# The gate of eight tokens a step moves from VectorE's one-hot columns into GpSimd's one-hot rows

## What is computed

```python
top_s, pos = lax.top_k(cand, PEER_TOPK)
eidx = jnp.take_along_axis(cidx, pos, axis=-1)          # i1 * 128 + i2
gate = jax.nn.softmax(top_s, axis=-1).astype(x.dtype)
...
hidden = jax.nn.gelu(jnp.einsum('td,thkd->thk', xb, u_tab[eb]))
return jnp.einsum('thk,thkd->td', gb * hidden, v_tab[eb])
```

## Time and profile before

| | |
|---|---|
| median of 3 runs | 3813.95 us (3813.29 to 3815.09) |
| the profiled execution | 3812.06 us |
| its span, first to last instruction | 3810.1 us |
| TensorE busy | 3728.1 us |
| VectorE busy | 2730.8 us |
| ScalarE busy | 1487.8 us |
| GpSimd busy | 1284.5 us |
| granted TensorE clock, mean | 0.996 |
| spreading stage, layer 1 | 953.0 to some 1097 us |
| spreading stage, layer 2 | 2846.2 to some 2991 us |

### The profile page before, as it was taken

How to read it: one execution, slowest core, us unless ns; L and a number is a source line. 1 busy time by engine, 2 the same in 40 slices (tenths; PEclk the granted TensorE clock), 3 DMA queues, 4 the chain that set the end, 5 groups by cost and what they waited for, 6 DMA issues and landing times. The chain is left out here.

```text
span 3810.1 us, 53339 instructions
## 1 busy us (share of the span) xinstructions
PE 3728.1 (98%) x19506; PEld 3310.0 (87%) x19506; DVE 2730.8 (72%) x5347; ACT 1487.8 (39%) x2154; POOL 1284.5 (34%) x1040
## 2 busy tenths in 40 slices
PE   8999999999999999999999999999999999999998
PEld 7878888999999999988878788889999899999887
DVE  3257635499989888878642566355999888888887
ACT  2244522244763333333322445223447533333332
POOL 1000000265856555544000000002658556555440
PEclk9999999999999999999999999999999999999999
DMA  4212423254689999999732225233537899999995
GB/s 148 101 56 75 161 91 138 108 184 157 216 287 382 358 355 348 344 346 354 257 133 94 65 68 171 78 139 112 206 142 229 302 378 357 358 350 344 342 357 208
DMA packets 321524, 847.59 MB, mean 222 GB/s; under 512 B 21056, under 2 KB 119360, under 8 KB 296256
## 3 DMA queue, kind: packets, MB, share of 16 engines
q1 hardware_dynamic: 247616, 576.84, 42.9%
q0 software_dynamic: 73728, 268.47, 18.8%
HBM read 755.58 MB, written 89.65 MB: 222 GB/s over the span
## 5 line engine op out<-in xcount | busy, mean ns | idle before, releaser
L93 PE MATMUL bank<-xT_low,u_high 128*128 128x384 f32 (+1 forms) x2144 | 728.9, 340 | 11.5 <-ACT hid L1897 7.3
L95 PE MATMUL bank<-xT_high,u_low 128*128 128x384 f32 (+1 forms) x2144 | 723.4, 337 | 0.0
L94 PE MATMUL bank<-xT_high,u_high 128*128 128x384 f32 (+1 forms) x2144 | 723.1, 337 | 0.0
L93 PE MATMUL bank<-v_low,w_high 128*128 128x512 f32 x1536 | 597.7, 389 | 0.9 <-DVE v_low L1998 0.9
L95 PE MATMUL bank<-v_high,w_low 128*128 128x512 f32 x1536 | 598.2, 389 | 0.0
L94 PE MATMUL bank<-v_high,w_high 128*128 128x512 f32 x1536 | 598.1, 389 | 0.0
L1189 POOL TENSOR_TENSOR u_low<-merged,u_high 128x1024 fp32r<-128x1024 f32 x96 | 243.1, 2546 | 1043.8 <-ACT u_high L1184 1043.6
L1257 POOL DMA_INDIRECT far_rows<-peer_v_dram,far_index x256 | 389.3, 1521 | 415.3 <-DVE x_far L1281 369.5
L1257 POOL DMA_INDIRECT far_rows<-peer_u_rows_dram,far_index x256 | 374.8, 1464 | 312.6 <-DVE far_dots L1263 259.7
L1998 DVE TENSOR_TENSOR v_low<-v_raw,v_high 128x1024 fp32r<-128x1024 f32 x256 | 301.8, 1221 | 207.4 <-ACT v_high L1909 207.3
L1909 ACT ACTIVATE v_high<-v_raw 128x1024 fp32r<-128x1024 f32 x256 | 257.3, 1052 | 472.2 <-PE bank L95 467.2
(11 more groups left out here) (445 smaller groups left out, 6811.3 us busy)
## 6 DMA issues: line engine op xcount, KB each, us to landing
merged<-peer_u_dram SPq DMA_DIRECT2D x128, 1024.0 KB, 7.7
v_raw<-peer_v_dram SPq DMA_DIRECT2D x128, 1024.0 KB, 9.4
gates_scratch<-stage SPq DMA_DIRECT2D x24, 2048.0 KB, 8.3
G<-gates_scratch SPq DMA_DIRECT2D x64, 768.0 KB
hidden_scratch<-ahead_hid SPq DMA_DIRECT2D x60, 384.0 KB, 2.6
hid<-hidden_scratch SPq DMA_DIRECT2D x30, 768.0 KB, 7.1
mg_raw<-w_merge_dram SPq DMA_DIRECT2D x28, 768.0 KB, 4.3
first_raw<-w_in_dram SPq DMA_DIRECT2D x20, 1024.0 KB, 5.6
```

The lines of the kernel that those rows point to most:

```text
L93: nc.tensor.matmul(out, lh, rl, start=first, stop=False)
L94: nc.tensor.matmul(out, lh, rh, start=False, stop=False)
L95: return nc.tensor.matmul(out, ll, rh, start=False, stop=last)
```

## The change

GpSimd's comparison of the rows of groups 2 and 3 gets a second scalar, the gate, and multiplies by it. VectorE's columns of those groups become plain comparisons; those of groups 0 and 1 keep the gate. The product is the same. No instruction is added, removed or moved, and no wait changes; each engine issues what it did, in the order it did. In the 48 steps of both layers this touches 384 instructions on GpSimd and 384 on VectorE.

```diff
                         for s in range(4 * g, 4 * g + 4):
-                            ins = nc.gpsimd.tensor_scalar(hot_row[:, s, :], iota_row[:], scalar_of(rowT, n, s), None, ALU.is_equal)
+                            ins = nc.gpsimd.tensor_scalar(hot_row[:, s, :], iota_row[:], scalar_of(rowT, n, s), scalar_of(gateT, n, s),
+                                                          ALU.is_equal, ALU.mult)
                         ins.then_inc(rows_hot, 1)
...
                         for s in range(4 * g, 4 * g + 4):
-                            ins = nc.vector.tensor_scalar(hot_col[:, n % 2, s, :], iota_row[:], scalar_of(colT, n, s), scalar_of(gateT, n, s),
-                                                          ALU.is_equal, ALU.mult)
+                            if g < 2:
+                                ins = nc.vector.tensor_scalar(hot_col[:, n % 2, s, :], iota_row[:], scalar_of(colT, n, s), scalar_of(gateT, n, s),
+                                                              ALU.is_equal, ALU.mult)
+                            else:
+                                ins = nc.vector.tensor_scalar(hot_col[:, n % 2, s, :], iota_row[:], scalar_of(colT, n, s), None, ALU.is_equal)
                         ins.then_inc(cols_hot, 1)
```

## The result

The change makes the kernel slower: 3877.19 us median (3874.09 to 3878.61) against 3814.44 for the kernel before, a ratio of 1.0165 with a 95% interval of 1.0152 to 1.0177. The forecast was 3850 in a range of 3806 to 3910; it had the direction and the new bound, and 36 us where 63 were measured.

A forecast was written before the change was run, and what follows sets the result against it. TensorE held the kernel; in the spreading stage, a loop of GpSimd's rows and a TensorE step. Afterwards GpSimd's sum, 13.36 against 11.83 us a period, gives + 33.7, last rows + 2.6: + 36.3, so 3850, range 3806 to 3910.

The forecast's parts named there:

- VectorE's relief: Eight column instructions a step lose the gate, saving VectorE 0.94 us a period; booked at nothing because columns are early.
- X: Extra time of each GpSimd row instruction for the gate and multiplication: 0.16 us, bounded by 0 and 0.39.
- the second operation: Part of a GpSimd row instruction's extra time: 0.10 us for 128 elements, at the rate of a write-only pass.
- the scalar: Part of a GpSimd row instruction's extra time: 0.06 us, VectorE's cost for a second scalar together with the second operation.
- contention: VectorE delaying GpSimd's rows, per period: 0.66 us beside plain comparisons and 0.86 beside the long subtraction.
- GpSimd's sum: Limit per two-step period of the spreading stage: 16 GpSimd instructions without a pause, 11.84 + 0.66 + 0.86 = 13.36 us.
- the loop: Spreading stage: eight GpSimd rows and a TensorE step wait on each other; 11.74 us a period before, 13.17 after.
- TensorE's 11.30: TensorE's own pace in the spreading stage without the gap before group 3: 5.65 us a step, 11.30 a period.
- Faster: Rival: VectorE's subtraction moves into GpSimd's pause, X small, the loop falls under TensorE's pace; 11.7 us won, 3802; chance 0.12.
- Cheap: Rival: GpSimd's gate costs only 0 to 0.08 us an instruction, still not faster, 3814 to 3830; chance 0.18.
- dear: Rival: GpSimd's gate costs above 0.30 us an instruction; 3900 at 0.30, 3934 at 0.39; chance 0.13.
- VectorE's time matters after all: Rival: a hidden column wait makes VectorE's saving count, - 0.94 us a period, at most - 11.7; part of 0.12.

The follow-up runs named there:

- e2: Changed kernel with GpSimd's row line put back, so only VectorE's columns of groups 2 and 3 become plain: 3818.8 us, 1.0013 of before.
- e7: Changed kernel with a second buffer for GpSimd's rows: 3870.7 us, 1.0148 of before.
- e8: Kernel before with a second buffer for GpSimd's rows and VectorE's columns of groups 2 and 3 plain, GpSimd's rows plain too: 3800.5 us, 0.9969 of before.
- e5: Kernel before with the gate moved from VectorE's columns to GpSimd's rows for group 3 only: 3840.4 us, 1.0071 of before.
- e6: Kernel before with a second buffer for GpSimd's rows, no gate moved: 3810.6 us, 0.9992 of before.
- e9: Kernel before with a second buffer for GpSimd's rows and VectorE's four plain comparisons for group 0 made in one instruction: 3802.0 us, 0.9970 of before.
- e3: Kernel before with GpSimd's rows given a second operation with a constant, times 1.0: 3848.2 us, 1.0094 of before.
- e4: Changed kernel with VectorE's column instructions left out from step 2 on: 3855.6 us, 1.0110 of before.

## Why the prediction was right, and where its size was off

**The direction and the new bound held.** GpSimd works without a pause and sets the pace, TensorE's busy share fell, VectorE has idle time, and the rest of the program kept its time, as the prediction said. Of its other signs, some came otherwise: a row instruction takes 0.918 us in the mean and not 0.84, the period is 14.4 and not 13.4, TensorE has its gaps ahead of group 3 alone and not of group 2, VectorE's idle time ends on ScalarE's `u_high` and not on matmuls, and the clock of the window is 0.97 and not 1.00. VectorE's relief booked at nothing: there is no gain from it in this kernel, by e2 (+ 5).

**X was too small.** Predicted 0.163, measured 0.199. Of the two parts, the second operation over 128 elements was 0.116 and not 0.103 (the rate of a write alone was its measure), the scalar 0.083 and not 0.06 (VectorE's price for both together). That is 0.036 x 16 x 22 + 0.036 x 8 x 2 = 13 us.

**The contention was too small.** Predicted 0.66 + 0.86 = 1.52 us a period. Measured: 14.40 - 16 x 0.776 = 1.98. The subtraction takes 0.97 and not 0.86. A column with two scalars, which I had taken as free, costs 0.05. Before it was free: a plain row instruction lasts 598 ns in the median beside such columns and 597 alone. It may be that its 577 ns fell in with two columns and one delay of VectorE (2 x 256 + 64 = 576 ns) and that 776 ns do not; no run tests that. The 0.46 us a period are 10 us in all. With the 13 above, the sum comes to 36.3 + 13.3 + 10.2 = 59.8 of the 62.8 measured. The 11.83 from which the forecast counted contains the slow first periods; from the steady 11.74 its sum would have been 2 us more. The last microsecond is left open.

**The two limits.** The prediction took the larger of GpSimd's sum (13.36) and the loop (13.17). That GpSimd's sum holds after the change is right: after the first steps it never pauses, and with the loop open (e7) the period stays. With the two so near each other, that the forecast named the right one owed something to luck. That the loop was the limit before rests on its own trace (TensorE 0.10 us behind GpSimd's last row in every odd step, with the columns 2.5 us early) and, with plain columns, on e8 against e2; e5, meant as its test, does not bear on it.

**A limit was missing.** The text put TensorE's 11.30 right behind the loop's 11.74. Between them was VectorE's own work, 11.69, which e6 uncovered. The prediction's reason, that VectorE "is always busy because it works ahead, up to two steps", was a misreading: its own rows have the columns only 1.3 to 2.5 us early, not a step or two of 5.9 us, and an engine that had used up its lead would have stood waiting for a buffer, which VectorE does not do once between 957 and 1090 us. It was busy because its work filled the period. "It is in nobody's way" was true only by some 0.05 us a period. It did not touch the forecast, since the change relieves VectorE, but a forecast for the second buffer alone, made by the same reading, missed by some 10 us.

**The rivals.** "Faster" wanted the subtraction to move into GpSimd's pause if X was small. e2 is that case at X = 0, and it was 5 us slower than before: the subtraction moved, but into the even step's rows, which are then in the loop, as the prediction held against this rival. So it falls even where its condition on X holds. "Cheap" (X up to 0.08) and "dear" (above 0.30) fall by X = 0.20. That VectorE's time matters after all is wrong of the change, and right of the kernel with two buffers and no gate moved (e6, e8).

## What to carry to other kernels

An engine that is busy all the time need not be the one that others wait for: look for who waits for it before paying another engine to relieve it. But if its results are only a little early and it never waits for a buffer, it isn't far ahead; it is the next limit. And an engine that pauses once a period for its own buffer can still be in the loop that holds the stage, so its pauses are no free room. A half dose (e5) did not tell the two apart here, because it used up the pauses; a second buffer did, once the next limit was out of the way (e2 against e8). When several engines run a stage at nearly the same pace, work moved between them may only change the name of the bound; open the loop (a second buffer) and take work away from the next limit, both together, as e9 does.

## What the runs showed of the hardware

- GpSimd's comparison of 128 float32 elements a partition with a scalar from memory: one every 0.577 us (before); with a second operation and a constant 0.693 (e3); with a second scalar from memory 0.776 (changed kernel). The first and the last of these on VectorE are some 0.20 and 0.26 us apart (before; medians 0.197 and 0.257).
- The two engines slow each other even where neither waits for a semaphore. VectorE's gated columns in the kernel before start 0.256 us apart at all 65 places where GpSimd has no instruction, and 0.284 in the mean beside one. GpSimd's gated row instruction of 0.79 us lasts 0.84 beside VectorE's two-scalar comparisons, 0.91 beside its one-scalar ones, and 1.76 beside a subtraction of two float32 tensors of 1024. Shorter neighbours hold it up longer than longer ones; why it is so no run here separates.
- Without VectorE's columns (e4) the changed kernel is 21.6 us faster than with them, with GpSimd's work unchanged.
